# Query and key blocks of a fused two-layer encoder: turned and moved in two steps, and differential score maps in two products

## The reference, cut to what matters

```python
h = rms_norm(x, pre_g)
parts = split(h @ w_in)                       # layer 0: 2048 x 8192, layer 1: 2048 x 12800
# layer 0: A = neighbourhood attention on the 4 x 64 grid with a learned bias, 8 heads
#          B = differential attention, 8 heads, partial rotary on q and k:
sc = einsum("bqhcd,bkhcd->bchqk", q, k) * 64 ** -0.5     # c = 0, 1: two halves of the head, 64 values each
p = softmax(sc); a = p[:, 0] - lam * p[:, 1]; o = rms_norm(a @ v, subln_g) * 0.8
# layer 1: C = windowed attention at dilations 1, 4 and 16, merged by their denominators, 3 x 8 heads
#          D = grouped-query attention, +-128 tokens, a sink per head, 8 heads on 2 key heads
x = x + rms_norm(concat(branches * silu(gates)) @ w_out, post_g)
```

## Time and profile before

| | us |
|---|---|
| median of 3 runs (range) | 1184.09 (1183.4 to 1186.24) |
| the profiled execution | 1184.91 |
| its span, first to last instruction | 1183.1 |
| TensorE busy in the span | 1164.0 (98%) |
| VectorE / ScalarE / GpSimd busy | 721.6 / 579.7 / 93.0 |
| granted TensorE clock | 0.998 of full |

### The profile page before, as it was taken

One profiled execution on the slowest core, in us unless ns is written; L12 is line 12 of the kernel. 1 busy time (PEld: TensorE's weight loads), 2 busy tenths in 40 slices (PEclk: granted clock), 3 DMA queues, 4 the chain that ended last, 5 costly groups with the idle time before them and its releaser, 6 DMA issues.

```text
span 1183.1 us, 14592 instructions
## 1 busy us (share of the span) xinstructions
PE 1164.0 (98%) x5492; PEld 971.4 (82%) x5492; DVE 721.6 (61%) x837; ACT 579.7 (49%) x756; POOL 93.0 (8%) x129
## 2 busy tenths in 40 slices
PE   7999999999999999999999999999999999999997
PEld 5777888888888888788888888888888888888886
DVE  5376556656665955764656555565746567658554
ACT  6545445544555644564545454444444444445442
POOL 2400002000000000010000101102011002000000
PEclk9999999999999999999999999999999999999999
DMA  9987766744646555455767666666766666454541
GB/s 365 260 235 278 226 224 210 231 174 147 244 153 243 178 198 194 145 211 177 237 218 227 220 205 224 211 220 204 239 200 191 228 205 212 144 205 149 202 150 72
DMA packets 77224, 244.18 MB, mean 206 GB/s; under 512 B 26048, under 2 KB 42560, under 8 KB 51696
## 3 DMA queue, kind: packets, MB, share of 16 engines
q1 hardware_dynamic: 74448, 233.87, 58.4%
q0 software_dynamic: 1856, 7.38, 2.4%
q10 hardware_dynamic: 864, 2.18, 0.5%
HBM read 223.47 MB, written 8.39 MB: 196 GB/s over the span
## 4 chain that ended last, share of the span: by engine, by line
PE 91%; DMA 4%; DVE 1%; ACT 1%; SPq 1%; issue 1%; ACTq 0%; DVEq 0%
PE acc L451 84%; PE bank_x L591 2%; DMA raw<-weights 2%; DMA probs<-x_nat 2%; PE bank_y L544 1%; SPq L319 1%; ACT w_hi L699 1%; PE bank_y L533 1%; PE bank_x L587 1%; PE bank_x L575 1%; PE bank_y L560 0%; PE bank_x L560 0%; PE bank_y L540 0%; PE bank_x L488 0%; PE bank_y L488 0%
## 5 line engine op out<-in xcount | busy, mean ns | idle before, releaser
L451 PE MATMUL acc<-w_hi,act_hi 128*128 128x512 f32 x1560 | 616.1, 395 | 2.3 <-DVE w_lo L979 2.0
L451 PE MATMUL acc<-w_lo,act_hi 128*128 128x512 f32 x1560 | 608.1, 390 | 0.0
L979 DVE TENSOR_TENSOR w_lo<-raw,w_hi 128x2048 fp32r<-128x2048 f32 x195 | 450.1, 2310 | 192.6 <-ACT w_hi L699 192.3
L699 ACT ACTIVATE w_hi<-raw 128x2048 fp32r<-128x2048 f32 x195 | 373.5, 1916 | 298.5 <-PE acc L451 273.4
L451 PE MATMUL acc<-w_hi,act_lo 128*128 128x512 f32 x1560 | 417.7, 389 | 0.0
L451 PEld LDWEIGHTS acc<-w_hi,act_lo 128*128 128x128 f32 x1560 | 292.7, 188 | 62.2 <-DVE act_lo L988 0.4
L451 PEld LDWEIGHTS acc<-w_hi,act_hi 128*128 128x128 f32 x1560 | 293.2, 188 | 61.4 <-DVE w_lo L979 3.9
L451 PEld LDWEIGHTS acc<-w_lo,act_hi 128*128 128x128 f32 x1560 | 293.3, 188 | 56.9
L706 ACT ACTIVATE unit<-acc,pre_r 128x512 f32<-128x512 f32 x78 | 49.3, 684 | 114.8 <-PE acc L451 114.4
L396 POOL TENSOR_TENSOR rope_c<-unit,cst 128x256 f32<-128x256 f32 (+1 forms) x19 | 14.1, 742 | 791.7 <-ACT unit L706 658.9
L721 ACT ACTIVATE probs<-scores,negm 128x256 f32<-128x256 f32 (+1 forms) x80 | 36.4, 458 | 31.0 <-DVE negm L1067 25.3
(11 more groups left out here) (168 smaller groups left out, 591.1 us busy)
## 6 DMA issues: line engine op xcount, KB each, us to landing
raw<-weights SPq DMA_DIRECT2D x195, 1024.0 KB, 5.0
qk_raw<-postg SPq DMA_DIRECT2D x176, 64.0 KB, 2.1
p_moved<-p_blocks SPq DMA_DIRECT2D x16, 256.0 KB, 5.5
probs<-p_moved SPq DMA_DIRECT2D x64, 64.0 KB, 2.0
resid<-x_turned SPq DMA_DIRECT2D x8, 256.0 KB, 9.2
mix<-rpb POOLq DMA_DIRECT2D x32, 64.0 KB, 23.7
postg<-post_g POOLq DMA_DIRECT2D x2, 1024.0 KB, 8.5
resid<-x_perm POOLq DMA_DIRECT2D x2, 1024.0 KB, 8.0
```

Source lines behind the costliest of these rows:

```text
L451: m = nc.tensor.matmul(tiles[t][:, :], a[:, kt, t * P:(t + 1) * P], w[:, buf, kk * NB:(kk + 1) * NB], start=(kt == 0 and a is act_hi and w ...
L699: nc.scalar.activation(w_hi[:, at % SPLIT, :], raw[:, at % RAW, :], ACT.Copy).then_inc(S["hi_ready"], 1)
L979: nc.vector.tensor_tensor(w_lo[:, at % SPLIT, :], raw[:, at % RAW, :], w_hi[:, at % SPLIT, :].bitcast(F32), ALU.subtract).then_inc(S["lo_r ...
```

## The change

Four things change.

- The turn and the gather are made by part. Queries are turned and moved in slot 6, keys in slot 10 (in the first body of each layer in slots 8 and 10). Each part has 16 DMAs of 32 KB, so a unit has 32 DMAs in place of 16, with counters `q_in` and `k_in`. The queries' and keys' regions in `postg` are separate halves.
- ScalarE waits for queries and keys by themselves in kinds A and W. In B and D the high parts are made one step earlier by name (step 1 for step 2); nothing stands between these two places in ScalarE's list.
- Differential maps: the stationary operand holds a half's high query parts in its 64 rows and the same queries' low parts in the other 64, which were zero. The moving operand holds that half's keys twice, high parts in one tensor and low parts in the other. A map is then 2 tiles x 2 products. ScalarE makes 6 copies per unit where it made 3, VectorE 6 subtractions where it made 3, in the same place ahead of the third chunk's split, half 0 first. The memset goes.
- Kind D: low parts at step 2 for step 3, the shared keys' transpose and split at step 3 for step 4.

```diff
-TURN = 10
-QK_DMAS = 16 * QUADS * QUADS
+TURNS = (6, 10)
+FIRST_TURNS = (8, 10)
+PART_DMAS = 16 * QUADS * QUADS
...
-            def gather(index):
-                sp.wait_ge(S["qk_turned"], index + 1)
+            def gather(index, blk):
+                sp.wait_ge(S[("q", "k")[blk] + "_turned"], index + 1)
                 for a in range(QUADS):
                     for j in range(QUADS):
-                        sp.dma_start(qk_raw[j * QUAD:(j + 1) * QUAD, a, :, :], blocks[a * QUAD:(a + 1) * QUAD, j, :, :]).then_inc(
-                            S["qk_in"], 16)
+                        sp.dma_start(qk_raw[j * QUAD:(j + 1) * QUAD, a, blk, :], blocks[blk][a * QUAD:(a + 1) * QUAD, j, :]).then_inc(
+                            S[("q", "k")[blk] + "_in"], 16)
...
-                        if s == TURN and turned_next(layer, u) is not None:
-                            gather(turned_next(layer, u))
+                        at = FIRST_TURNS if u is None else TURNS
+                        if s in at and turned_next(layer, u) is not None:
+                            gather(turned_next(layer, u), at.index(s))
                         load(CHUNK0[layer] + BODY * b + s + 2 + RAW, i)
...
-                    for n, (a, b) in enumerate(PARTS):
+                    for part in range(2):
                         m = nc.tensor.matmul((Y, X)[c][:, t * SEQ:(t + 1) * SEQ].rearrange("p (t a c) -> p t a c", t=NT, a=QUADS),
-                                             split_q[:, c, a, t * UH + j, :],
-                                             keys_of((k_hi[:, :, :], k_lo)[b], j), start=(n == 0), stop=(n == len(PARTS) - 1))
+                                             q_hi[:, c, t * UH + j, :], keys_of(both_k[:, c, part, :, :], j),
+                                             start=(part == 0), stop=(part == 1))
...
+                act.wait_ge(S["q_in"], PART_DMAS * u.index + PART_DMAS)
+                if u.kind != "A" and u.kind != "W":
+                    act.wait_ge(S["k_in"], PART_DMAS * u.index + PART_DMAS)
                 if u.kind == "B":
                     for c in range(2):
+                        mine, other = (slice(64 * r, 64 * r + 64) for r in (c, 1 - c))
+                        nc.scalar.activation(by_quads(q_hi[mine, c, :, :]), raw_quads(0, mine), ACT.Copy).then_inc(S["qk_hi"], 1)
+                        nc.scalar.activation(both_k[other, c, 0, :, :], qk_raw[mine, :, 1, :], ACT.Copy)
+                        nc.scalar.activation(both_k[mine, c, 0, :, :], qk_raw[mine, :, 1, :], ACT.Copy).then_inc(S["qk_hi"], 1)
...
+            def turn_part(layer, index, blk):
...
+                nc.vector.transpose(blocks[blk][:, :, :].rearrange("p j (n c) -> p j n c", c=QUAD),
+                                    unit[:, blk, :, :].rearrange("p t (h j c) -> p j (t h) c", j=QUADS, c=QUAD)).then_inc(
+                    S[("q", "k")[blk] + "_turned"], 1)
+            def split_both_lo(u, c):
+                mine, other = (slice(64 * r, 64 * r + 64) for r in (c, 1 - c))
+                dve.wait_ge(S["qk_hi"], hi_count(u) + 2 * c + 1)
+                nc.vector.tensor_tensor(by_quads(q_hi[other, c, :, :]), raw_quads(0, mine),
+                                        by_quads(q_hi[mine, c, :, :].bitcast(F32)), ALU.subtract)
+                dve.wait_ge(S["qk_hi"], hi_count(u) + 2 * c + 2)
+                for rows in (other, mine):
+                    m = nc.vector.tensor_tensor(both_k[rows, c, 1, :, :], qk_raw[mine, :, 1, :],
+                                                both_k[mine, c, 0, :, :].bitcast(F32), ALU.subtract)
+                m.then_inc(S["qk_ready"], 1)
...
-                if h == 3 and u.kind != "G":
+                if u.kind == "B" and h in (2, 3):
+                    split_both_lo(u, h - 2)
+                if h == (2 if u.kind == "D" else 3) and u.kind not in ("B", "G"):
                     split_qk_lo(u)
```

More of the change, by code:

```diff
@@ L150, in build @@
         mix = sb("mix", [P, NT, D_MODEL])
-        with nc.sbuf_tensor("split_q", [P, 2, 2, NT * UH, P], F32R) as split_q:
+        with nc.sbuf_tensor("both_k", [P, 2, 2, QUADS, NT * UH * QUAD], F32R) as both_k:
             pass
@@ L223, in build @@
         unit_out_flat = unit_out[:, :, :].rearrange("p t n -> p (t n)")
-        blocks = postg[:, :].rearrange("p (j b n) -> p j b n", j=QUADS, b=2)
+        blocks = [postg[:, at:at + 1024].rearrange("p (j n) -> p j n", j=QUADS) for at in (1024, 0)]
         acc = [[ctx.enter_context(nc.psum_tensor(f"acc{s}_{t}", [P, NB], F32)) for t in range(NT)]
@@ L240, in build @@
                  "y_sq y_scaled y_sum y_var y_std y_rdy "
-                 "rs_v rs_s rs_rdy tanh_done gate_u gate_done q_zeroed").split()
+                 "rs_v rs_s rs_rdy tanh_done gate_u gate_done").split()
         S = {n: sem(n) for n in names}
@@ L278, in turned_next, with hi_count @@
             return None if u is not None and (u.kind == "D" or layer == 0 and at == end) else at
+        def hi_count(u):
+            return 2 * split_units(u) + (0 if u.kind == "A" else 2 * (u.index - 2) if u.kind == "B" else 4)
         def split_units(u):
@@ L416, in _ @@
                         rotate(u, k, blk, cols, HEAD // 2 if layer == 0 else HEAD)
[L417 to L421, removed]
                 if layer == 0:
-                    pool.wait_ge(S["qk_in"], QK_DMAS * UNITS[0])
+                    pool.wait_ge(S["q_in"], PART_DMAS * UNITS[0])
+                    pool.wait_ge(S["k_in"], PART_DMAS * UNITS[0])
                     pool.dma_start(postg[:, :], post_g[0].partition_broadcast(P)).then_inc(S["postg_in"], 16)
@@ L597, in attention @@
                     return
-                if u.kind == "D" and h == 4:
+                if u.kind == "D" and h == 3:
                     turn_shared_k(u)
@@ L740, in split_qk_hi @@
             def split_qk_hi(u):
[L742 removed]
+                act.wait_ge(S["q_in"], PART_DMAS * u.index + PART_DMAS)
+                if u.kind != "A" and u.kind != "W":
+                    act.wait_ge(S["k_in"], PART_DMAS * u.index + PART_DMAS)
                 if u.kind == "B":
[L745 removed]
                     for c in range(2):
[L747 to L749 removed]
+                        mine, other = (slice(64 * r, 64 * r + 64) for r in (c, 1 - c))
+                        nc.scalar.activation(by_quads(q_hi[mine, c, :, :]), raw_quads(0, mine), ACT.Copy).then_inc(S["qk_hi"], 1)
+                        nc.scalar.activation(both_k[other, c, 0, :, :], qk_raw[mine, :, 1, :], ACT.Copy)
+                        nc.scalar.activation(both_k[mine, c, 0, :, :], qk_raw[mine, :, 1, :], ACT.Copy).then_inc(S["qk_hi"], 1)
+                    return
                 elif u.kind == "G":
@@ L775, in attention @@
                         order_pT(u, j)
-                if h == 2:
+                if h == (1 if u.kind in ("B", "D") else 2):
                     split_qk_hi(u)
-                if h == 4 and u.kind == "D":
+                if h == 3 and u.kind == "D":
                     act.wait_ge(S["k_full"], 1)
@@ L1011, in turned @@
                 m.then_inc(S["turn_taken"], 1)
-            def turn_qk(layer, index):
+            def turn_part(layer, index, blk):
                 if layer == 0 and index < 2:
-                    dve.wait_ge(S["proj_ready"], PROJ0[0] + 3 * index + 2)
+                    dve.wait_ge(S["proj_ready"], PROJ0[0] + 3 * index + 1 + blk)
                 else:
-                    dve.wait_ge(S["roped"], CREDIT + 2 * (index - 2) + 2)
-                for blk in range(2):
-                    m = nc.vector.transpose(blocks[:, :, blk, :].rearrange("p j (n c) -> p j n c", c=QUAD),
-                                            unit[:, blk, :, :].rearrange("p t (h j c) -> p j (t h) c", j=QUADS, c=QUAD))
-                m.then_inc(S["qk_turned"], 1)
@@ L1025, in split_qk_lo @@
[L1025 to L1035, removed]
+                    dve.wait_ge(S["roped"], CREDIT + 2 * (index - 2) + 1 + blk)
@@ L1036, in split_qk_lo @@
+            def split_qk_lo(u):
+                dve.wait_ge(S["k_in"], PART_DMAS * u.index + PART_DMAS)
+                for blk in range(2):
+                    dve.wait_ge(S["qk_hi"], hi_count(u) + blk + 1)
+                    if blk == 0 or u.kind == "D":
                         m = nc.vector.tensor_tensor(by_quads(q_lo[:, blk, :, :]), raw_quads(blk),
@@ L1313, in _ @@
                             turned(16 * layer + 2 * s + 2, layer)
-                        if s == TURN and turned_next(layer, u) is not None:
-                            turn_qk(layer, turned_next(layer, u))
+                        at = FIRST_TURNS if u is None else TURNS
+                        if s in at and turned_next(layer, u) is not None:
+                            turn_part(layer, turned_next(layer, u), at.index(s))
                         split_lo(CHUNK0[layer] + BODY * b + s + 2, i)
```

7 lines of the change are left out of this document (4 added, 3 removed).

## The result

| | before | changed |
|---|---|---|
| median of the runs | 1184.83 us (1183.40 to 1186.24, 4 runs) | 1217.66 us (1210.79 to 1222.06, 4 runs) |
| span of the profiled execution | 1183.1 us | 1217.2 us |
| granted TensorE clock over the span | 0.998 | 0.989 |

The changed kernel takes 1.0267 times as long, with an interval of 1.0242 to 1.0292: slower by some 33 us, where 15 were forecast. The forecast's sign and its chain of causes came out; the size did not, and the time lies outside the range of 1181 to 1208.

The account below looks back on a forecast made before the run. TensorE, busy for 98% of the span, was taken as the bound. -3.8 - 1.6 + 18.3 + 2.1 = +15.0 us on the profiled 1184.9 gave 1199.9, stated as 1199 us; range 1181 to 1208.

Parts of the forecast that it names:

- The forecast's sign: Whole kernel: slower, by 15.0 us, with chance 0.81.
- its chain of causes: Slot 6: the queries' gather holds SyncE's queue, head 2's move starts some 9 us late, TensorE waits in eight units.
- What bounds the kernel: Whole kernel: TensorE, busy for 98% of the span, so the time is the sum of its instructions.
- the products (-3.8): Differential maps: two products fewer in each of 16 maps, 32 at 0.12 us, all on the path.
- SyncE's queue in slot 6 (+18.3): A, W and G units: 10.0 us gather ahead of head 2's move; eight TensorE waits of 1.8 to 2.9 us.
- Head 3 has no second wait: Same units: head 3's move is pushed back too, but lands in time with little over 1 us of cover.
- Rival 3: TensorE's eight new idle stretches bring the granted clock down, 2 us each: 1215 us; chance 0.05.
- The wait goes: -1.6 us: First unit: keys' gather starts sooner, 2.2 us gained against the 1.6 us wait before the first scores; later loads cost nothing.
- The differential units (+2.1): B units: extra copies and subtractions delay the start; TensorE waits 1.8 us in the second, 0.3 in the first.
- Costs at nothing: Memset, place of the splits, D's shared keys wanted 2.7 us sooner, loads behind a gather: no cost, at most tenths in D.

Follow-up runs that it names:

- experiment 5: Second kernel of experiment 4 with the first unit's query issues spread over slots 6 to 9: 1183.34 us; second kernel, each differential-map product also done twice: 1190.56 us.
- experiment 1: Kernel before the change plus 12, 16, 18 or 22 extra SyncE issues in slot 6 of eight units: 1185.27, 1197.14, 1214.72, 1246.9 us.
- experiment 4: Changed kernel, query issues in SyncE's waits, B units' query parts before keys: 1186.27 us; second kernel, also first unit's queries in slot 6, not 8: 1186.08 us.
- experiment 2: Changed kernel with both turns in slot 10 and one gather of sixteen 64 KB issues, as before the change: 1185.18 us.

## Why the prediction was right and wrong, step by step

- **What bounds the kernel; the products (-3.8).** Right. A map in the changed kernel runs from 326.70 to the next product at 327.18, 0.48 us as forecast, and experiment 5 confirms the price.
```profile
326.70 0.64 PE L562 MATMUL bank_y<-both_k,q_hi 128*128 128x256 f32 x4
327.18 0.40 PE L453 MATMUL acc<-w_hi,act_hi 128*128 128x512 f32 x1
```
- **SyncE's queue in slot 6 (+18.3).** Right in mechanism, place and nearly in size: 20.7. The gather takes 10.02 us as forecast. Before, head 2's write started 2.85 us after its last score instruction (118.28 to 121.13); now it is 11.87 us (120.52 to 132.39), so 9.0 us later, the forecast's number. A, A, W, W: forecast 2.4, 2.9, 2.6, 2.5, measured 2.5, 3.8, 3.2, 2.5; G: 2.3, 1.8, 1.9, 1.9 against 2.9, 1.8, 2.2, 1.8. Head 3 has no second wait, as forecast.
- **Rival 3, "The clock", is the step that failed.** It was priced at 2 us for each unit, 16 in all, and given 0.05, since "the 1.6 us wait left no mark on a clock of 0.998". The row was read correctly, but a single wait of 1.6 us says little about eight of 1.8 to 3.8: five of them were followed by half rate, 10.6 us in all. As priced, the rival came near: its 1215 is the forecast with 16 us of clock on top. What failed is that the forecast's sum took the clock at nothing, so that the range left it out as well. With the term, 1199.9 + 10.6 = 1210.5 would have been near the shortest run (1210.79). In experiment 1 the waits bring half rate without any of the change's other edits: after three of eight with 18 issues, after all eight with 22.
- **"The wait goes: -1.6 us" failed too (+1.4).** Compare with SyncE's timeline at the changed kernel's start:
```profile
63.91 10.12 SPq L324 DMA_DIRECT2D qk_raw<-postg  x16
74.07 1.06 SPq L317 DMA_DIRECT2D raw<-weights  x2
75.17 10.01 SPq L324 DMA_DIRECT2D qk_raw<-postg  x16
```
The keys' issues did start sooner, by 0.6 us (75.17 against 75.73). But the forecast asked only whether the loads behind the queries would be late for TensorE, and priced that at nothing. It didn't ask what they would do to the transfers behind them: two loads of 1 MB now go out right ahead of the keys. The keys' last issue ended at 85.18 and low q, which waits for them, began only at 91.31; before, the first copy after the landing began 87.99. That these two loads are the cause is not shown. The wait before the first scores scatters: 0.5 to 2.3 us in the six kernels that keep the old gather at the start, 3.0, 4.8 and 1.2 us in the three that have the changed start, none in the second kernel of experiment 4 and the first of experiment 5, but 1.7 us in the second of experiment 5, which has the same start as the first. In that one the keys landed some 6.5 us after their last issue (84.1 to 90.7) though no load stood behind more than four issues; in the changed kernel it took 6.1. What makes the landing late stays open; the rows only show that the wait did not go in the changed kernel, because the keys landed at 91.3, and not sooner than before.
```profile
91.31 1.23 DVE L1049 TENSOR_TENSOR q_lo<-qk_raw,q_hi 128x1024 fp32r<-128x1024 f32 x1 [1.96 <-DMA qk_raw<-postg]
```
- **The differential units (+2.1).** Nearly right: 1.1 and 0.5 us, all in the second B unit. Its copies and low parts cost 1.06 and 1.22 us each, as forecast, in series behind the landing; that unit's wait was for the keys (2.96 us), which agrees with experiment 4, where letting the queries go first removed the wait.
```profile
319.38 1.06 ACT L751 ACTIVATE q_hi<-qk_raw 64x1024 fp32r<-64x1024 f32 x1 [2.96 <-DMA qk_raw<-postg]
320.47 1.06 ACT L752 ACTIVATE both_k<-qk_raw 64x1024 fp32r<-64x1024 f32 x1
```
- **Costs at nothing.** The shared keys of unit D and the memset: no wait at either place, as forecast. The waits on `w_lo` at the start, +1.2 us, stood in no term; in the six kernels that keep the old gather at the start they come to 2.0 to 3.5 us there from one profiled execution to the next, so part of it is scatter.

From +15.0 to +34.1: clock 10.6, first unit 3.0, the eight waits 2.4, start 1.2, B units -0.5, restart and unexplained 2.4.

## What to carry to other kernels

Price a moved transfer by its number of issues times the issue's own time on that queue, and look at what stands behind it on two sides: the instructions that wait for the queue, and the transfers that the held-back loads will now run into (their price is not settled here). When a forecast adds TensorE waits of some 2 us or more, add the clock to the sum as a term with a range, and not as a rival outside it: here from nothing to 3.4 us for each wait (half of a 6.8 us stretch). One wait in the trace of before that left the clock whole doesn't price it at nothing. Issues that don't fit in front of a wait of the queue's own may be free inside it.

## What the hardware showed that was not expected

- The granted clock fell to half for 3.4 or 6.8 us at a time. Of the 32 unit waits in four kernels, none of the eight up to 2.0 us with 16 extra issues was followed by it; with 18, those of 1.85, 2.41 and 2.51 were, and those of 1.77, 1.95, 2.90, 2.99 and 3.05 were not; in the changed kernel those of 2.5 to 3.8 were, and those of 1.8, 1.8 and 2.2 were not; with 22, all eight of 4.5 to 5.7 were. At the start, 3.0 us before the first scores was not followed by it in the changed kernel, while 2.3 us at the same place in experiment 2 was. Between 1.8 and 3.1 us the length of a wait doesn't decide. What does is not shown.
- An issue from SBUF to SBUF on SyncE has a median of 591 ns at 16, 32 and 64 KB alike, all with 32 partitions at either end.
- From 16 to 18 extra issues per unit, 1.2 us of the queue in each, the time rose by 17.6 us, nearly twice the waits: the trace has 9.4 of them, 5.1 of half rate behind them, and 3.4 of half rate at the start, where no extra issue stands.
